# Moving weight splits into the attention loop and a row sum into the middle of a unit, in a two-layer hybrid decoder trunk

## The reference

```python
h = rms_norm(x, norm_mix_pre[l])
(c_q, c_kv, k_rope, ml_q, ml_k, ml_v, ml_o, ml_i, ml_f, sw_q, sw_k, sw_v) = jnp.split(h @ w_in[l], splits, axis=-1)
y_a = mla_mixer(...)          # 8 heads, causal
y_b = mlstm_mixer(...)        # 4 heads of matrix memory, output gate sigmoid(o)
y_c = dilated_swa_mixer(...)  # 4 heads
y = jnp.concatenate([y_a, y_b, y_c], axis=-1) @ w_out[l]
x = x + rms_norm(y, norm_mix_post[l])
h = rms_norm(x, norm_x_pre[l])
y = memory_cross_attention(h, rms_norm(mem, norm_mem[l]), x_w_q[l], x_w_kv[l], x_w_o[l])
x = x + rms_norm(y, norm_x_post[l])
h = rms_norm(x, norm_ffn_pre[l])
y = swiglu(h, w_gate_up[l], w_down[l])
x = x + rms_norm(y, norm_ffn_post[l])
```

## Time and profile before

| | |
|---|---|
| median of 3 runs | 1653.46 us (1652.97 to 1655.12) |
| the profiled execution, its own time | 1652.96 us |
| its span in the profile | 1651.2 us |
| PE busy | 1582.8 us, 96% |
| DVE busy | 896.1 us, 54% |
| ACT busy | 720.6 us, 44% |
| POOL busy | 20.1 us, 1% |
| mean granted clock of TensorE | 0.994 |

### The profile page before, as it was taken

One profiled execution on the slowest core, in us unless ns is written; L12 is line 12 of the kernel. 1 busy time (PEld: TensorE's weight loads), 2 busy tenths in 40 slices (PEclk: granted clock), 3 DMA queues, 4 the chain that ended last, 5 costly groups with the idle time before them and its releaser, 6 DMA issues.

```text
span 1651.2 us, 18993 instructions
## 1 busy us (share of the span) xinstructions
PE 1582.8 (96%) x7428; PEld 1242.7 (75%) x7428; DVE 896.1 (54%) x1384; ACT 720.6 (44%) x1216; POOL 20.1 (1%) x26
## 2 busy tenths in 40 slices
PE   6999899999999999999999989999999999999996
PEld 5776568976778888888777655788867788888884
DVE  4866645845375555542278666458445555555322
ACT  4634644624444444432255356456244444444320
POOL 0000010000000000000000001000000000000000
PEclk9999999999999999999999999999999999999998
DMA  6221003520322333333322210135202323233221
GB/s 233 90 77 46 20 5 130 185 92 24 95 84 90 94 98 102 90 102 92 100 77 77 64 52 1 65 123 158 90 27 76 102 90 102 96 96 102 90 90 51
DMA packets 38536, 143.45 MB, mean 87 GB/s; under 512 B 4272, under 2 KB 4400, under 8 KB 37936
## 3 DMA queue, kind: packets, MB, share of 16 engines
q1 hardware_dynamic: 38448, 142.25, 26.9%
HBM read 140.13 MB, written 2.10 MB: 86 GB/s over the span
## 4 chain that ended last, share of the span: by engine, by line
PE 87%; DVE 6%; ACT 4%; issue 2%; DMA 1%; SPq 0%; DVEq 0%; ACTq 0%
PE bank L566 24%; PE bank L568 23%; PE bank L567 23%; PE bank L847 2%; PE bank L877 2%; PE bank L955 2%; PE bank L945 2%; PE bank L653 1%; PE bank L864 1%; PE bank L654 1%; PE bank L657 1%; PE bank L787 1%; ACT w_hi L1024 1%; PE bank L776 1%; DVE w_lo L1412 1%
## 5 line engine op out<-in xcount | busy, mean ns | idle before, releaser
L1412 DVE TENSOR_TENSOR w_lo<-raw,w_hi 128x1024 fp32r<-128x1024 f32 x254 | 310.5, 1225 | 389.4 <-ACT w_hi L1024 387.0
L566 PE MATMUL bank<-h_hi,w_hi 128*128 128x512 f32 x1216 | 484.6, 399 | 21.9 <-DVE w_lo L1412 10.6
L567 PE MATMUL bank<-h_lo,w_hi 128*128 128x512 f32 x1216 | 475.6, 391 | 0.0
L568 PE MATMUL bank<-h_hi,w_lo 128*128 128x512 f32 x1216 | 475.4, 391 | 0.0
L1024 ACT ACTIVATE w_hi<-raw 128x1024 fp32r<-128x1024 f32 x254 | 266.0, 1051 | 188.1 <-DMA raw<-w_in 181.1
L566 PEld LDWEIGHTS bank<-h_hi,w_hi 128*128 128x128 f32 x1216 | 229.4, 189 | 80.9 <-issue 23.2
L567 PEld LDWEIGHTS bank<-h_lo,w_hi 128*128 128x128 f32 x1216 | 229.6, 189 | 50.2 <-issue 3.4
L568 PEld LDWEIGHTS bank<-h_hi,w_lo 128*128 128x128 f32 x1216 | 229.5, 189 | 48.3
L566 PE MATMUL bank<-a_hi,w_hi 128*128 128x512 f32 x352 | 137.1, 389 | 0.0
L568 PE MATMUL bank<-a_hi,w_lo 128*128 128x512 f32 x352 | 137.0, 389 | 0.0
L567 PE MATMUL bank<-a_lo,w_hi 128*128 128x512 f32 x352 | 136.9, 389 | 0.0
(11 more groups left out here) (215 smaller groups left out, 2017.5 us busy)
## 6 DMA issues: line engine op xcount, KB each, us to landing
raw<-w_in SPq DMA_DIRECT2D x254, 512.0 KB, 3.6
x<-x_in SPq DMA_DIRECT2D x4, 512.0 KB, 8.2
mem<-mem_in SPq DMA_DIRECT2D x2, 1024.0 KB, 4.9
out<-x SPq DMA_DIRECT2D x4, 512.0 KB, 2.6
consts<-c_in SPq DMA_DIRECT2D x1, 1600.0 KB, 12.9
mem_sq<-mem_in SPq DMA_DIRECT2D x1, 1024.0 KB, 16.3
gains<-g_in SPq DMA_DIRECT2D x1, 80.0 KB, 3.6
```

Of the source, the lines that this page charges most:

```text
L566: pe.matmul(out_ap, l_hi, r_hi, start=start, stop=False)
L567: pe.matmul(out_ap, l_hi, r_lo, start=False, stop=False)
L568: return pe.matmul(out_ap, l_lo, r_hi, start=False, stop=stop)
L1412: dve.tensor_tensor(w_lo[:, s, :], raw[:, s, :], w_hi[:, s, :].bitcast(F32), ALU.subtract)\
```

## The change

Three things are moved; no operation is added, removed or resized.

1. Splits of the units 31 and 32, the fifth and sixth of the output projection. Unit 31 was split at the end of the mLSTM (at the end of `uv`), unit 32 in the output projection's second step. Now `split_until(U_OUT + AHEAD)` stands at s == 4 and `split_until(U_OUT + AHEAD + 1)` at s == 7 on ACT, and the `lo_until` to them at s == 5 and s == 8 on DVE.
2. The hi and lo parts of the last mLSTM output: from s == 1 to s == 10 on ACT and to s == 11 on DVE.
3. Row sums. `norm_sum("mix_pre")` goes ahead of the k-step 4 of the unit that follows the head, and the four transposes one unit further than the head: in layer 0 the sum goes from before unit 3 to its middle and the transposes from behind unit 3 to behind unit 4; in layer 1 the sum goes from behind unit 4 to its middle and the transposes stay. `norm_sum("ffn_pre")` goes from behind unit i == 4 to its middle, in both layers.

The hunks below are, in order: PE's input projection, PE's feed-forward, ACT at the end of the mLSTM and in the attention, DVE in the same two places.

```diff
+SUM_STEP = 4
...
                     pe.wait_ge(consts_loaded, 16)
-                    if layer:
-                        project("in", head, tiles(h_hi), tiles(h_lo))
-                        head += 1
-                    norm_sum("mix_pre")
+                    def sum_inside(k):
+                        if k == SUM_STEP:
+                            norm_sum("mix_pre")
                     for m in range(head, IN_FM):
-                        project("in", m, tiles(h_hi), tiles(h_lo))
-                        if m == head:
+                        project("in", m, tiles(h_hi), tiles(h_lo), before=sum_inside if m == head else None)
+                        if m == head + 1:
                             pe.wait_ge(rstd_ready, count(rstd_ready, layer, 1))
...
                         for i in (2 * p, 2 * p + 1):
-                            if i == 5:
-                                norm_sum("ffn_pre")
...
                             for k in range(KT):
+                                if i == 4 and k == SUM_STEP:
+                                    norm_sum("ffn_pre")
                                 mm = gate_up_step(i, k)
...
-                            if ended(name, m):
+                            if ended(name, m) and name != "uv":
                                 split_until(ended(name, m) + AHEAD)
...
-                        if s == 1:
+                        if s in (BATCHES + 1, 2 * BATCHES + 1):
+                            split_until(U_OUT + AHEAD - 1 + s // BATCHES)
+                        if s == 3 * BATCHES + 1:
                             ml_output_hi(1)
...
-                            if ended(name, m):
+                            if ended(name, m) and name != "uv":
                                 lo_until(ended(name, m) + AHEAD)
...
-                        if s == 1:
+                        if s in (BATCHES + 2, 2 * BATCHES + 2):
+                            lo_until(U_OUT + AHEAD - 1 + s // BATCHES)
+                        if s == 3 * BATCHES + 2:
                             ml_output_lo(1)
```

## The result

| | before | after |
|---|---|---|
| median | 1653.57 us (1652.97 to 1655.12, 4 runs) | 1640.77 us (1639.65 to 1641.42, 4 runs) |
| the profiled execution, its own time | 1652.96 us | 1641.42 us |
| its span | 1651.2 us | 1639.6 us |

A forecast was written before the change was run, and what follows sets the result against it. PE, busy 96% of the span, bounds the kernel, so only its gaps can be won. -7.4 - 5.1 - 2.7 + 1.3 = -13.9 from 1652.96 gives 1639.0, 1639.3 with half the offset to the median; range 1636.2 to 1644.

The forecast's parts named there:

- attention, both layers: Start of the attention: PE's waits for masks and for DVE's copy shrink or vanish, 3.7 us per layer on average, 7.4 in all.
- moved parts where they stand now: Attention pairs: splits and mLSTM output parts cost nothing, since ACT waited 3.76 us and DVE 2.62 us for PE there.
- row sum, feed-forward: Sum 2.72 us earlier lets the seventh unit's split end before PE asks; gap closes, 2.57 us per layer, 5.1 in all.
- row sum, input projection, layer 1: Sum 2.72 us earlier starts DVE's whole stretch earlier, so PE starts the tokens' projection earlier: 2.7 us won.
- row sum, input projection, layer 0: Sum 2.72 us later delays unit 4's split; PE gets a new gap of 1.2 us: 1.3 us lost.
- Both gaps: Attention start: PE's 2.2 us gap ahead of the third batch's scores shrinks to 0.5; its 1.97 us copy wait goes.
- The rival "slower": Attention: moved parts land on the critical path, adding 11.8 us and losing the 7.4 gained: 1658 us; chance 3%.
- the first gap's fall of the clock: Layer 1's input projection, 864 to 868: half rate costing some 1.6 us should vanish with its gap, hidden by DVE's chain.
- the second fall: Layer 1's input projection, 891 to 895: half rate behind the longer gap, some 1.6 us lost, was to stay.
- a rival of 14%: Layer 0's new gap or layer 1's longer one costs another half-rate stretch, 1.6 to 3.2 us: 1641 to 1642.5; chance 14%.
- its two places: Input projection: layer 0's new 1.2 us gap and layer 1's longer gap of about 4 us, where half rate might follow.
- a fall belongs to a gap: PE's clock: idle time is paid twice, so each new or longer gap could bring half rate after it, though not every wait.

The follow-up runs named there:

- the fastest version: Changed kernel with the input projection's row sum ahead of k-step 0 behind the head units in both layers, layer 0's transposes back as before: 1634.06 us, ratio 0.988.

## Why the prediction was right

1639.3 was predicted and 1640.77 measured, within the range, faster as given 0.93. Term by term in us; "alone" is the run with that part alone:

| term | predicted | in the change's trace | alone |
|---|---|---|---|
| attention, both layers | -7.4 | -3.54, -3.41 | -3.55, -3.37 |
| moved parts where they stand now | 0 | 0 | 0 even with all three in one pair |
| row sum, feed-forward | -5.1 | -2.63, -2.63 | -2.60, -2.65 |
| row sum, input projection, layer 1 | -2.7 | -2.71 | -2.72 |
| row sum, input projection, layer 0 | +1.3 | +1.29 | +1.27 |
| sum | -13.9 | -13.6 | |

**Attention.** Both gaps closed by the mechanism given, and the runs with one moved thing each show which holds which. The 0.26 us that layer 0 lacks lie at its very start: I laid DVE's first mask at 172.2, straight behind the scores, and in the clock of before it starts at 172.46 (174.06 less 1.60); everything behind it is as much later.

**The cost of nothing** was right, and by more than I claimed: the prediction counted DVE's own wait (1.4 us left) as the cover, and the run with all in one pair used it up and still lost nothing. The place mattered, though: one step earlier a third and more of the gain is gone. The rival "slower" never came near.

**Layer 1's projection.** The prediction said that the first gap's fall of the clock was hidden by DVE's chain. Ten traces have that gap, at 1.83 or 1.84 us. Where no fall follows it, PE waits 4.5 us at the take of unit 9 (three traces), where one follows 2.8 to 3.1 (six), where a double one follows 1.63 (one): the fall is paid out of the next wait, as claimed.

**The clock** is where the prediction was wrong in its mechanism, though it cost little here. It took the second fall as it was and gave a rival of 14% to a part taken back by it. In the profiled execution that rival came true, with 1.57 us at 142 to 148 and 1.20 behind the 3.63 us gap; but the first of these was not one of its two places, and a second execution had neither. What failed is the step "a fall belongs to a gap": after which of the gaps a fall comes changes from execution to execution, and how many come in all depends on which gaps the kernel has (mean granted clock 0.9914 with only the splits moved, 0.9955 with the sum at the head). That the median came within 1.5 us of the forecast is in this part luck. The Trainium skill, TensorE: Matmul & The Clock Gate, "What's actually happening", has the clock follow how busy the array has recently been; the falls agree in that none of these traces shows one in the body of the kernel without waits of PE of about 0.8 us or more in it or just ahead, but no row tells beforehand after which of them it comes.

The first pair of traces adds up: -13.6 by the places, -1.2 by the start, +1.57 and +1.20 by the clock, +0.5 by a longer wait of the cross-attention's projection for `h_lo` (1.25 us at 333.95, 0.71 before), together -11.5 for a span that is 11.6 shorter. That the medians differ by 12.8 and not 13.6 is less than these executions scatter; the ratio's interval is 10.7 to 15.7 us.

## What to carry to other kernels

Work on an engine that isn't the bottleneck is free where that engine waits for the bottleneck, and also where what it does next isn't asked for yet; so look for who waits for the *following* instruction, and take the place a step earlier or later as another place. A link that a whole chain hangs on (a row sum) is worth its distance until the chain's gap is closed, which one timeline tells in advance: undo it where the chain wasn't late (layer 0 here, 1.3 us) and move it further where a gap remains (layer 1, 2.7 us more). Read gains of 1 or 2 us from starts of the same instruction in two traces, and take a second profiled execution before a stretch at half rate is put down to an edit. Look at the mean granted clock of all executions too: a gap that is closed can be paid back to the clock (the splits alone).

## What was unexpected of the hardware

The falls of TensorE's clock come in one size: each stretch at 1.2 GHz costs up to 1.7 us against 2.4 GHz, if PE is busy through it (one minus the granted clock, times 2, summed over the 2 us windows of a stretch: 1.7 in 28 stretches, 3.4 in five). Over the fourteen traces of this case, the kernel before and the changed one twice each, from 20 us to the last matmul:

| PE's gap ahead | places | followed by a fall |
|---|---|---|
| 3.6 to 4.5 us, take of unit 9, layer 1 | 6 | 6 (three of them double) |
| 2.8 to 3.1 us, same place | 6 | 3 (one double) |
| 2.33 us, feed-forward | 16 | 10 |
| 1.83 us, unit 6, layer 1 | 10 | 7 (one double) |
| 1.9 to 2.1 us, one or two in an attention | 16 | 4 |
| 1.2 to 1.5 us, cross-attention's projection for `h_lo` | 4 | 0 |
| 0.9 + 0.8 us, at the `sw` rotations (1.5 us follow) | 28 | 3 |
| 1.02 us, unit 4, layer 0, where the sum is moved | 3 | 0 |
| 0.97 us, feed-forward (sum at k-step 6) | 2 | 0 |

A closed gap of 2.33 us is thus worth its 2.6 us and, on average, a further 1.7 x 10/16 = 1.1 us (an estimate; the medians of the two runs that close both such gaps and nothing else are 6.1 and 7.9 us below the kernel before beside them, 3.0 and 3.9 a gap). The same scatter makes executions of one kernel differ: 1652.0 to 1656.6 us in the eleven runs of the projection's sum alone, and only 1633.6 to 1634.6 in the four runs of the fastest version, which has the fewest gaps left.

The start varies in the same way. The first 512-column matmuls start 0.43 us apart, as they do in the stretches at a granted clock of 0.50, and from some point on 0.23. The windows give 1.00 there throughout, but only because they count time without a record of the clock as full: the first record in the trace is the rise, at 21.52 us in the kernel before and 20.17 in the changed one. The matmuls at that place, in the one and the other:

```profile
20.91 0.63 PE L567 MATMUL bank<-h_lo,w_hi 128*128 128x512 f32 x1
21.33 0.48 PE L568 MATMUL bank<-h_hi,w_lo 128*128 128x512 f32 x1
21.66 0.40 PE L566 MATMUL bank<-h_hi,w_hi 128*128 128x512 f32 x1
```

```profile
19.84 0.56 PE L568 MATMUL bank<-h_lo,w_hi 128*128 128x512 f32 x1
20.23 0.40 PE L569 MATMUL bank<-h_hi,w_lo 128*128 128x512 f32 x1
```

In the second trace of each the rise is at 19.15 and at 18.38. The first matmul itself, released by loads and splits, starts between 7.97 and 9.13 in these four. Together they put the first row sum of the kernel before at 33.95 in one execution and 32.32 in the other; so a stretch's gain is to be taken over the stretch, not from the span.
